# A four-layer transformer stack on one core: waits by name at the attentions' beginnings and ends, and more products of halves in the first layer

## The reference

```python
h, gate = _modulate(x, c, norm_g, w_ada, b_ada)            # rmsnorm(x) * (1 + scale) + shift
hc, gate_c = _modulate(xc, c_ctx[None, :], norm_g, w_ada, b_ada)
qa, ka, va, qb, kb, vb, g = _split(h @ w_in, EVEN_SPLITS)  # 512,128,128,512,512,512,1024 columns
...                                                        # the same for hc
ya = _window_gqa_sink(rope(qa), rope(ka), va, kac, vac, a_sink)
yb = rmsnorm(diff_attend(rope(qb), [rope(kb); kbc], [vb; vbc], lam)) * (1 - lam_init)
y = concat(ya, yb) * silu(g)
x = x + gate * (y @ w_out)
```

## Time and profile before

| | |
|---|---|
| time of 3 runs | median 2337.09 us (2337.0 to 2337.59) |
| the profiled execution's own time | 2341.98 us |
| its span | 2340.2 us |
| mean granted clock of PE | 0.994 |
| PE busy | 2274.7 us (97%) |
| DVE, ACT, POOL busy | 1309.9 (56%), 795.4 (34%), 326.5 us (14%) |
| mean DMA rate | 97 GB/s |

### The profile page before, as it was taken

How to read it: one execution, slowest core, us unless ns; L and a number is a source line. 1 busy time by engine, 2 the same in 40 slices (tenths; PEclk the granted TensorE clock), 3 DMA queues, 4 the chain that set the end, 5 groups by cost and what they waited for, 6 DMA issues and landing times. The chain is left out here.

```text
span 2340.2 us, 30852 instructions
## 1 busy us (share of the span) xinstructions
PE 2274.7 (97%) x11976; PEld 1732.8 (74%) x11976; DVE 1309.9 (56%) x2919; ACT 795.4 (34%) x1707; POOL 326.5 (14%) x349
## 2 busy tenths in 40 slices
PE   7999999999999999999999999999999999999998
PEld 5866576678546657688866888887787678888876
DVE  3565565764246644757768476664368855433334
ACT  4255103531013203723548122223443652222333
POOL 2200110010000111021100110003543001000154
PEclk9999999999999999999999999999999999999999
DMA  7200331002234363013210255554321102322322
GB/s 311 73 19 22 124 108 63 19 28 75 92 122 130 97 192 103 1 63 121 97 48 2 70 182 180 181 193 130 108 84 71 55 1 99 133 92 90 108 91 81
DMA packets 58270, 225.92 MB, mean 97 GB/s; under 512 B 20478, under 2 KB 21118, under 8 KB 41740
## 3 DMA queue, kind: packets, MB, share of 16 engines
q1 hardware_dynamic: 58124, 223.94, 28.3%
HBM read 221.83 MB, written 2.10 MB: 96 GB/s over the span
## 5 line engine op out<-in xcount | busy, mean ns | idle before, releaser
L86 PE MATMUL PS<-Hr,GBr 128*128 128x512 f32 (+1 forms) x1332 | 440.6, 384 | 0.6 <-DVE RINGr L103 0.6
L86 PE MATMUL PS<-Hr,RINGr 128*128 128x512 f32 (+1 forms) x1112 | 410.0, 373 | 0.0
L96 ACT ACTIVATE WK<-PS 128x512 f32<-128x512 f32 (+2 forms) x391 | 189.2, 516 | 459.2 <-PE PS L86 279.5
L86 PE MATMUL PS<-H,RING 128*128 128x512 f32 (+1 forms) x928 | 338.3, 517 | 1.9 <-DVE GB L115 1.9
L115 DVE SCALAR_TENSOR_TENSOR ACC<-ADA,SM,ACC 128x256 f32<-128x256 f32 x608 | 293.8, 506 | 48.1 <-DMA ADA<-in_l_mod 28.5
L86 PEld LDWEIGHTS PS<-Hr,GBr 128*128 128x128 f32 x1332 | 247.7, 188 | 51.7 <-issue 3.9
L86 PEld LDWEIGHTS PS<-H,RING 128*128 128x128 f32 x928 | 172.6, 191 | 138.7 <-issue 128.3
L103 DVE TENSOR_TENSOR RINGr<-RING,GBr 128x1024 fp32r<-128x1024 f32 x148 | 182.8, 1273 | 148.5 <-ACT GBr L96 148.1
L86 PE MATMUL PS<-RING,GB 128*128 128x256 f32 x1152 | 253.3, 381 | 3.4 <-DVE GB L120 2.2
L86 PEld LDWEIGHTS PS<-RING,GB 128*128 128x128 f32 x1152 | 219.1, 191 | 34.6 <-issue 5.0
L86 PEld LDWEIGHTS PS<-Hr,RINGr 128*128 128x128 f32 x1112 | 208.9, 188 | 38.0
(11 more groups left out here) (222 smaller groups left out, 2828.9 us busy)
## 6 DMA issues: line engine op xcount, KB each, us to landing
ADA<-in_l_mod SPq DMA_DIRECT2D x96, 512.0 KB, 3.7
RING<-in_l_gu SPq DMA_DIRECT2D x44, 1024.0 KB, 4.9
RING<-in_l_wd SPq DMA_DIRECT2D x24, 1024.0 KB, 4.9
RING<-in_ev_in SPq DMA_DIRECT2D x13, 1024.0 KB, 5.8
ADA<-in_od_ada SPq DMA_DIRECT2D x24, 512.0 KB, 3.6
RING<-in_od_in SPq DMA_DIRECT2D x11, 1024.0 KB, 6.2
RING<-in_l_in SPq DMA_DIRECT2D x10, 1024.0 KB, 5.1
RING<-in_l_out SPq DMA_DIRECT2D x8, 1024.0 KB, 4.8
```

Of the source, the lines that this page charges most:

```text
L86: self.last = self.eng.matmul(out, lhsT, rhs, start=start, stop=stop, skip_group_check=True)
L96: self.last = self.eng.activation(out, in_, func, bias=bias, scale=scale)
```

## The change

1. `_is_split` takes chunks 0 to 8. Chunks 3 to 8 (gates 0 to 3, qb, kb) are rounded and multiplied as three products. ACT rounds 3, 4, 5 in steps 2, 4, 16 of attention A, and 6, 7, 8 in projection B ahead of the rotation of qb 0, qb 2, kb 0; POOL forms the rests of 3, 4, 5 in attention A and of 6, 7, 8 at qb 0, qb 2, kb 0.
2. The sums H = Hh + Hl leave attention A. They are made after the last product of kb 3, k 0 and 1 by DVE, ahead of its rotation of kb 2, and k 2 to 7 by POOL. vb(0) goes over k outside and its six tiles inside, in three banks of two tiles each, all taken before its first matmul; all its copies wait for its last. vb(0)'s tiles 0, 1, 4, 5 are ACT's, 2, 3 DVE's.
3. Attentions B, N, S, D begin without waiting for the copies of the last products: `close` stands ahead of these, and PE waits for them by name at step 2 (B, N, D) or 0 (S); in projection M `close` stands ahead of the copies of gates 4 to 7. After attentions N, S and D, PE waits for each k by name (`outputs`) instead of `since`. DVE's copies of vd(1) 4 and 5 come ahead of the maxima of their step.
4. `ada_until(ADA_AFTER["od", 3])` before out ev is gone, and out ev's first call is `ada(4)`: that step of the list, and the calls behind it, come one call later.
5. In a ffn, ACT's `round_a(0)` and `(1)` come at gu chunks 20 and 21, POOL's part at chunk 21.

The diff, cut to its core:

```diff
 def _is_split(i):
-    return PLAN[i][0] in SPLIT or PLAN[i][0] == "ev_in" and PLAN[i][1] < 3
+    return PLAN[i][0] in SPLIT or i < 9
...
+            def values_by_feature(i, tag):
+                W = ring_view(i, 8)
+                pe.wait_ge(ring_in[i % NRING], ("ring", i))
+                for t in range(0, 6, 2):
+                    where["p", tag, t + 1, 0] = next_bank(("p", tag, t, 0), copied(tag, t, 0) + copied(tag, t + 1, 0))
+                for k in range(8):
+                    wait_h("whole", k, 0)
+                    for t in range(6):
+                        at = t % 2 * 256
+                        pe.matmul(bank(where["p", tag, t, 0], at, at + 256), Ht(k, t * 128, (t + 1) * 128), W[:, k, :],
+                                  k == 0 and t % 2 == 0, k == 7)
...
+            def outputs(tags, lru=False):
+                by = {U["done"][0]: attended_by(tag, u, U) for tag in tags for u, U in enumerate(UNITS[tag]) if U["done"]}
...
-                        fm(i, 8, m, tag, t, roped(tag, t), ALLT, Ht, whole, rotate)
+                        fm_split("ev", i, m, tag, t, roped(tag, t), ALLT, rotate)
                         ada(4)
                     chunk_done(i)
...
+            values_by_feature(9, ("vb", 0))
+            ada(4)
...
-            ada_until(ADA_AFTER["od", 3])
...
-                     lambda t: ada(3) if t < 4 else norm_mod("od", [(0, range(4))], by_h) if t == 4 else None, True)
+                     lambda t: ada(3 + (t == 0)) if t < 4 else norm_mod("od", [(0, range(4))], by_h) if t == 4 else None, True)
...
-            since(pe, "att N")
...
-            out_proj("od_out", range(4), lambda k, t: None, then_l0m)
+            out_proj("od_out", range(4), outputs("MN"), then_l0m)
...
 # vector: projection B
+                    if tag == "kb" and t == 3:
+                        dve.wait_ge(pe_product, ("p", "kb", 3, 512))
+                        for k in range(2):
+                            dve.tensor_tensor(Ht(k), Hh("ev", k, 0, 768), Hl("ev", k, 0, 768), ALU.add)
+                            dve.then_inc(dve_value, ("whole", k))
+                        own(("whole", 1))
+                        rope("kb", 2, ALLT)
...
 # gpsimd: projection B
+                    if t % 2 == 0 and q * 2 + t // 2 < 3:
+                        rest(6 + q * 2 + t // 2)
                     rope(tag, t)
                     ada(4)
+            for k in range(2, 8):
+                own()
+                pool.wait_ge(pe_product, ("p", "kb", 3, 512))
+                pool.tensor_tensor(Ht(k), Hh("ev", k, 0, 768), Hl("ev", k, 0, 768), ALU.add)
```

More of the change, by code:

```diff
@@ L455, in hi_place @@
             name, s = PLAN[i][0], _side(i)
-            if i == 2:
+            if i in (2, 4):
                 place = GATEr[:, h * 1024:h * 1024 + 1024]
+            elif i in (3, 5, 7):
+                place = GBr[:, 3072 + h * 1024:4096 + h * 1024]
             elif name == "ev_in":
@@ L830, in program, with whole_signal @@
         gates_t, wi_t = WK[0:24, 5120:5632], WK[0:8, 6656:7040]
+        def whole_signal(k):
+            return dve_value if k < 2 else pool_value
         def product(tag, t, s0, n):
+            if tag == ("vb", 0):
+                return bank(where["p", tag, t, s0], t % 2 * 256, t % 2 * 256 + n)
             return bank(where["p", tag, t, s0], 0, n)
@@ L1011, in tm @@
                     pe.then_inc(pe_product, ("p", tag, t, 0))
+            def values_by_feature(i, tag):
[9 more added lines that the diff above has]
+                                  k == 0 and t % 2 == 0, k == 7)
+                for t in range(6):
+                    pe_product.at["p", tag, t, 0] = pe_product.n + 1
+                pe.then_inc(pe_product)
             def copied(tag, t, s0):
@@ L1087, in gate_part @@
                     where["p", "ga", t, s0] = 7
-                W = ring_view(i, 8)
-                pe.wait_ge(ring_in[i % NRING], ("ring", i))
                 for k in range(2 * part, 2 * part + 2) if part < 4 else range(4 * part - 16, 4 * part - 12):
+                    if t < 4:
+                        (Wh, Wl), c = split_weights(i, 8), slice(t % 2 * 128, t % 2 * 128 + 128)
+                        pe.wait_ge(rest_signal(i), ("rest", i, k // 4))
+                        wait_h("ev", k, part // 4)
+                        hh, hl = Hh("ev", k, s0, s0 + n), Hl("ev", k, s0, s0 + n)
+                        pe.matmul(bank(7, 0, n), Wh(k, c), hh, k == 0, False)
+                        pe.matmul(bank(7, 0, n), Wh(k, c), hl, False, False)
+                        pe.matmul(bank(7, 0, n), Wl(k, c), hh, False, k == 7)
+                        continue
+                    W = ring_view(i, 8)
+                    pe.wait_ge(ring_in[i % NRING], ("ring", i))
                     wait_h("whole", k, 0)
@@ L1354, in at_end, with values_b @@
                 sub_norms(i)
-            attention("B", None, at_end)
+            def values_b(i):
+                for t in range(6) if i == 2 else ():
+                    for s, event in copied(("vb", 1), t, 0):
+                        pe.wait_ge(s, event)
+            attention("B", values_b, at_end)
             turn["set"] = list(range(2, 8))
@@ L1444, in values_d @@
                     chunk_done(i)
+                elif z == 2:
+                    for t in range(4):
+                        for s, event in copied(("vd", 1), t, 0):
+                            pe.wait_ge(s, event)
                 elif z == 10:
@@ L1565, in values_s @@
                         chunk_done(FIRST["l0_in4"] + 1)
+                for t in range(2) if i == 0 else ():
+                    for s, event in copied("ks", t, 0):
+                        pe.wait_ge(s, event)
                 for t in V0_BY.get(i, ()):
@@ L1577, in then_l0f @@
                     norm_early("l0f")
-            out_proj("l0_out", range(4), lambda k, t: None, then_l0f)
+            out_proj("l0_out", range(4), outputs("S", True), then_l0f)
             cur.allowed |= {"l1m"}
@@ L1646, in tensor, with last_queries @@
             since(pe, "proj D")
-            attention("D")
+            def last_queries(i):
+                for t in (6, 7) if i == 2 else ():
+                    for s, event in copied("q1", t, 0):
+                        pe.wait_ge(s, event)
+            attention("D", last_queries)
             ada_until(ADA_AFTER["l1m", 5])
             close(of_pe, "att D")
-            since(pe, "att D")
-            out_proj("l1_out", range(4), lambda k, t: None, lambda t: norm_early("l1f") if t == 2 else None)
+            out_proj("l1_out", range(4), outputs("D"), lambda t: norm_early("l1f") if t == 2 else None)
             close(of_pe, "out l1")
@@ L1925, in values_a @@
                     copy_out("va", t, 0, 128)
+                for ahead in {2: (3,), 4: (4,), 16: (5,)}.get(i, ()):
+                    round_chunk(ahead)
             attention("A", values_a)
@@ L3123, in ffn, with lower_a @@
                 close(of_pool, "norm " + st)
-                for f in range(22):
-                    ada(FFN_STEPS[st])
-                ada_until(ADA_AFTER[st, 5])
-                for fz in range(40):
+                def lower_a(fz):
                     own()
@@ L3133, in ffn @@
                     pool.then_inc(pool_value, ("al", wd, fz))
+                for f in range(22):
+                    if f == 21:
+                        lower_a(0)
+                        lower_a(1)
+                    ada(FFN_STEPS[st])
+                ada_until(ADA_AFTER[st, 5])
+                for fz in range(2, 40):
+                    lower_a(fz)
                 for t in range(4):
@@ L3155, in gpsimd @@
             since(pool, "proj A")
+            for i in (3, 4, 5):
+                rest(i)
             close(of_pool, "att A")
```

106 lines of the change are left out of this document (58 added, 48 removed).

## The result

The changed kernel takes 2318.74 us (median of 4 runs, 2318.04 to 2320.4), the kernel before 2337.34 beside it: a ratio of 0.9927, 95% interval 0.9914 to 0.994, 18.6 us less. The forecast was 2318 with 2303 to 2328.

The account below looks back on a forecast made before the run. PE, busy for 97% of the span, was taken as the bound, so only less matmul time or PE idle helps. Terms -7.9 -15.9 +7.1 +11 -8.3 -4.3 +0 = -18.3 off 2337.09 gave 2318 us, range 2303 to 2328.

Parts of the forecast that it names:

- eight tiles at 1.98 less: Projection B: eight tiles multiplied as three products, each 1.98 us shorter than unsplit, 15.9 us less in all.
- the wait before vb(0): End of projection B: PE stalls for DVE's late sums and rotation of kb 2 beside POOL's sums, 11 us more.
- 7.1 us for the modulation's sums: Projection B: POOL's rests make DVE late, so PE waits 4.0 us behind qb 2 and 3.1 behind kb 0.
- Attention A, 7.9: Attention A: sums gone (-2.65), gates' pieces shorter (-7.5), ACT's rounding (+1.3) and POOL's rests (+1.0): 7.9 us less.
- The clock, taken as 0: PE's clock falls behind waits: 1.7 us saved by falls that go, 1.7 added by a new stall, 0 in all.
- The modulation's shift, 1.6: Before out ev: PE's wait of 1.55 us for the sum of od 3 goes, 1.6 us less; other moved waits 0.
- The named waits, 8.3: Starts of attentions B, S, D, ends of N, S, D, and N's transposes: PE's waits for copies go, 8.3 us less.
- The ffn, 2.7: First wd product of ffn l0: PE's wait for a(0)'s rounding and rest goes, 2.7 us less; ffn l1 0.
- (a): Projection B: POOL hardly disturbs DVE, as its operations fall where DVE waits or reads PSUM: 2306 us, chance 0.25.
- (c): Attention borders: naming waits changes nothing, first units need the same late copy, so 8.3 becomes 3: 2323 us, chance 0.10.
- (d): Projection B: DVE holds POOL up too, so PE loses more at rests and sums: 2351 us at full price, chance 0.05.
- (b): PE's clock: new stalls in projection B bring half speed behind each, and old falls stay: 2323 us, chance 0.12.

Follow-up runs that it names:

- e1: The changed kernel with ACT copying the high halves of k 2 to 7 in place of POOL's six sums: 2311.83 us, ratio 0.9889 to the kernel before.
- e2: The changed kernel with ACT writing zeros in place of POOL's rests of chunks 6, 7, 8: 2310.55 us, ratio 0.9884 to the kernel before.
- e9: The kernel before with only the named waits at the attentions' beginnings and ends and DVE's earlier copies of vd(1): 2326.61 us, ratio 0.9953.
- e3: The kernel before with only parts 1 and 2 of the change (products of halves, sums, vb(0) by feature): 2338.5 us, ratio 1.0004.
- e10_shift_only: The kernel before with only the modulation's shift by one call, from out ev on: 2325.83 us, ratio 0.995.

## Why the prediction was right, and where it was not

- *What bounds the kernel; eight tiles at 1.98 less.* Right: 9.20 us from rotation to rotation.
- *DVE stands while POOL works, and the wait before vb(0).* Right in kind and place, and mis-sized: I took 11 of a range of 6.1 to 15; it is 14.55. The lower end, what DVE's order alone costs, was 6.1 and measured 5.23 in e1; it had 1.5 for DVE being late, which it was not (e2). That POOL's sums stand full length against DVE was the upper end, and rows 7 had shown it; there was no reason to go below it. That copies out of PSUM do not stand did not shorten it, since they queue behind the two sums.
- *7.1 us for the modulation's sums.* At the places named it is 3.63 (4.0 forecast) and 1.44 (3.1): 5.1, and all of it the rests' (e2).
- *Attention A, 7.9.* By the shift of qb 0's rotation (11.8, less 1.4 from the start of the kernel, less that tile's own 2.0) it gained 8.4, so the number was right in part by luck: 1.7 of it is a fall of the clock behind the wait of 1.62 (0.93 over 120 to 130 us and 0.90 over 130 to 140 before, 1.00 in both after), which I had not counted, and e9, which keeps the wait (1.63), is without it as well. The block of 1.88 us was inside my +1.0 for the rests, too little; the waits of 1.03 and 1.62 became 0.17 and, with one of 0.62 for ACT, 0.44.
- *The clock, taken as 0.* This step failed, twice. In the changed kernel the clock falls behind each of the three new waits: 8.1 us in projection B where I had 1.7. And of the falls of the kernel before behind 1.62, 1.55, 1.33, 2.31 and 2.71 us none is left, where I had counted one at most. (The price of 1.7 a fall holds, though rows 14 by themselves give 0.37 x 3.4 = 1.3: the fall outlasts their windows, and over 1600 to 1610 us the clock is 0.83.)
- *The modulation's shift, 1.6.* This step failed by the most: 12.2 alone, 9.3 within the whole change. I priced the one wait that the edit was beside and took the shift of all later calls as zero between two small bounds. The list sets waits of PE up to ffn l0, and I did not ask of the waits in norm l0m, norm l0f and ffn l0 which call each belongs to.
- *The named waits, 8.3.* 11.4 alone. The idle of the rows went as forecast, the end of S excepted in e9 (0.79 stays until the other edits move a list step away); the rest is falls of the clock that e9 does not have, some of them at places that no name touches.
- *The ffn, 2.7.* Nothing, once the list is shifted.
- Sum for sum: parts 1 and 2 were to bring 5.7 and bring nothing (-1.2 to +3.0 us by the interval of e3); parts 3 to 5 were to bring 12.6 and bring 20. The two errors cancel by luck, and 2318 came out for partly wrong reasons.
- *The rivals.* (a), POOL hardly disturbs DVE, is refuted by e1 and e2, (c), the names change nothing, by e9. (d), POOL held up as well, did not come: 1.94 and 2.6 us an operation (244.47: 5.26 for two), with the one exception of 2.84 at 240.22. (b) has its half: the new falls came, but the old ones went too.

## What to carry to other kernels

Work with two inputs in SBUF that was given to GpSimd beside a busy VectorE cost VectorE about the length of GpSimd's instruction here, not nothing: two subtractions of 1.2 us a chunk on VectorE itself were 10.8 us cheaper over three chunks than the same on GpSimd at 2.6 each, falls of the clock included. Price it so, or place it where VectorE waits or reads PSUM. When an in-order list of side work is moved by one call, look up every wait that one of its steps sets over the whole run, not the one beside the edit; and test two groups of edits apart even when the sum comes out as forecast.

## What the runs showed of the hardware that was not expected

The clock's fall does not follow from the length of a wait. The plainest case is in code that no edit touches: behind the same wait of 1.83 us, at 48.5 us, it falls in the kernel before (first window) and not in the changed one (second):

```profile
50.00:55.00 5.00, 5.00 (x16) 3.95 (x15) 2.62 (x3) 1.74 (x2) 0.85 (x1) 0.66 0.05 20
50.00:55.00 5.00, 5.00 (x26) 4.20 (x25) 2.88 (x3) 2.35 (x4) 0.88 (x1) 1.00 0.03 11
```

Behind 1.55 us in e9_names_only it falls (first of the next windows), behind 2.31 and 2.71 us in the same execution it doesn't (second and third):

```profile
510.50:514.50 4.00, 3.99 (x19) 3.76 (x20) 0.65 (x4) 0.00 (x0) 0.00 (x0) 0.62 0.36 135
1051.40:1055.00 3.60, 3.57 (x31) 3.57 (x32) 3.46 (x6) 1.45 (x4) 0.86 (x3) 1.00 0.26 77
1591.50:1595.10 3.60, 3.60 (x16) 2.99 (x17) 3.39 (x6) 1.43 (x2) 1.26 (x1) 1.00 0.64 210
```

The kernel before fell behind both of the latter waits, and did not behind its 2.20 us in attention N, where e10_shift_only, with the same wait of 2.21, did:

```profile
914.20:918.20 4.00, 4.00 (x17) 2.07 (x17) 1.16 (x3) 2.91 (x6) 0.00 (x0) 0.61 0.64 121
```

So a wait of 1.3 to 2.7 us costs itself, and in some executions 1.7 us more. What decides which was not settled by these runs. Each kernel was profiled in one execution, so where the falls lie in its other runs is not known. The Trainium skill, "TensorE: Matmul & The Clock Gate", section "What's actually happening", says that the throttled state is the default one and that activity releases it; the longest wait agrees, with 0.50 for the 5 us behind it.

The other surprise is how small a VectorE instruction can be and still stand: 128x1 elements, 2.35 us beside GpSimd.
